# Expert stage of a two-block transformer kernel: all heads of row 0 first, then row 1, each expert choice for one row

## The reference

```
q = (hf @ wq).reshape(t, 8, 2, 128)
sc = einsum('thpd,hpnd->thpn', q, sub_keys)           # 2 x 128 scores for each head
top_v, top_i = top_k(sc, 16)
cand = top_v[:, :, 0, :, None] + top_v[:, :, 1, None, :]    # 16 x 16 candidates
best_v, best_pos = top_k(cand, 16)
expert_id = take_along_axis(top_i0 * 128 + top_i1, best_pos)
gate = softmax(best_v)
# for each token, head and each of the 16 experts chosen:
act = gelu(einsum('phkd,pd->phk', u_table[expert_id], x))
out = einsum('phk,phkd->pd', gate * act, v_table[expert_id])
# then: x = x + out, and a last rmsnorm
```

## Time and profile before

| | us |
|---|---|
| median of 3 runs | 1723.84 |
| the profiled execution | 1718.18 |
| its span in the trace | 1716.9 |
| first gather issued | 1024.46 |
| last gather issued | 1686.90 |
| TensorE / VectorE / ScalarE / GpSimd busy | 1513.6 / 1071.8 / 683.0 / 351.6 |

### The profile page before, as it was taken

The page is one execution under the profiler, slowest core; times in us unless marked ns, Lnnn a source line. Parts: engine busy times, 40 slices in busy tenths (PEclk is TensorE's granted clock), DMA queues, the critical chain, the costliest instruction groups (busy, mean ns, idle before and its releaser), DMA issues.

```text
span 1716.9 us, 21093 instructions
## 1 busy us (share of the span) xinstructions
PE 1513.6 (88%) x7772; PEld 1113.7 (65%) x7772; DVE 1071.8 (62%) x1906; ACT 683.0 (40%) x1512; POOL 351.6 (20%) x325
## 2 busy tenths in 40 slices
PE   3999989998989997998999998788797888887886
PEld 3899988898889997888996774443342434332322
DVE  6666675875665556668454236486776767667645
ACT  2434445344354444643342213334434434343433
POOL 1100010000010001002100013344444444444431
PEclk8999999999999998989999999999999999999999
DMA  9777756664655554332334439989899999999996
GB/s 361 273 246 252 241 189 239 222 204 164 219 170 185 186 187 142 94 97 95 98 99 172 172 104 418 384 318 423 361 422 421 421 422 421 421 421 421 420 422 264
DMA packets 90856, 463.12 MB, mean 270 GB/s; under 512 B 10752, under 2 KB 10912, under 8 KB 57728
## 3 DMA queue, kind: packets, MB, share of 16 engines
q0 software_dynamic: 39216, 277.05, 39.3%
q1 hardware_dynamic: 50688, 183.52, 31.7%
q10 hardware_dynamic: 848, 1.18, 0.2%
HBM read 459.62 MB, written 2.10 MB: 269 GB/s over the span
## 4 chain that ended last, share of the span: by engine, by line
PE 60%; DMA 18%; DVE 13%; ACT 5%; issue 3%; POOL 1%; SPq 0%; DVEq 0%; ACTq 0%; POOLq 0%
DMA Ft<-peer_uv,ids 14%; PE ps L1220 9%; PE ps L460 7%; PE ps L461 7%; PE ps L462 7%; DVE Ft L1982 3%; PE ps L1052 3%; PE ps L1137 3%; PE ps L576 2%; PE ps L577 2%; PE ps L578 2%; DMA mlo<-peer_uv,ids 2%; DVE wlo L1243 2%; PE ps L504 2%; PE ps L505 2%
## 5 line engine op out<-in xcount | busy, mean ns | idle before, releaser
L1220 PE MATMUL ps<-Ft 128*128 128x512 f32 x796 | 385.3, 618 | 81.7 <-ACT Ft L2505 81.1
L1220 PEld LDWEIGHTS ps<-Ft 128*128 128x128 f32 x796 | 145.0, 194 | 306.1 <-ACT Ft L2505 174.6
L1243 DVE TENSOR_TENSOR wlo<-raw,whi 128x1024 fp32r<-128x1024 f32 x228 | 277.9, 1244 | 69.0 <-ACT whi L2006 68.6
L460 PE MATMUL ps<-uhi,whi 128*128 128x256 f32 x1088 | 314.2, 289 | 6.6 <-DVE ulo L1331 6.0
L1982 DVE CUSTOM_DVE_ANT_0 Ft<-Ft 128x1024 f32<-128x1024 f32 x199 | 243.9, 1226 | 116.9 <-DMA Ft<-peer_uv,ids 108.6
L461 PE MATMUL ps<-ulo,whi 128*128 128x256 f32 x1088 | 310.7, 286 | 0.0
L462 PE MATMUL ps<-uhi,wlo 128*128 128x256 f32 x1088 | 310.3, 285 | 0.0
L2627 POOL DMA_INDIRECT Ft<-peer_uv,ids x199 | 221.0, 1111 | 314.4 <-PE ps L1220 241.7
L2006 ACT ACTIVATE whi<-raw 128x1024 fp32r<-128x1024 f32 x228 | 229.7, 1048 | 27.7 <-DMA raw<-ff_gu 15.7
L460 PEld LDWEIGHTS ps<-uhi,whi 128*128 128x128 f32 x1088 | 211.7, 195 | 10.5 <-issue 8.3
L461 PEld LDWEIGHTS ps<-ulo,whi 128*128 128x128 f32 x1088 | 211.6, 194 | 1.9 <-issue 0.5
(11 more groups left out here) (411 smaller groups left out, 2177.1 us busy)
## 6 DMA issues: line engine op xcount, KB each, us to landing
raw<-ff_gu SPq DMA_DIRECT2D x88, 512.0 KB, 4.7
raw<-w_ada SPq DMA_DIRECT2D x72, 512.0 KB, 5.0
raw<-ff_dn SPq DMA_DIRECT2D x44, 512.0 KB, 4.5
raw<-w_in SPq DMA_DIRECT2D x32, 512.0 KB, 3.7
raw<-w_in_s SPq DMA_DIRECT2D x28, 512.0 KB, 4.2
raw<-w_out SPq DMA_DIRECT2D x14, 512.0 KB, 4.6
raw<-w_in_m SPq DMA_DIRECT2D x12, 512.0 KB, 4.6
raw<-xa_wk SPq DMA_DIRECT2D x8, 512.0 KB, 3.6
```

The costliest lines, as they stand in the source:

```text
L460: t.matmul(o, hi[:, c], x[0][:, i], start=(k == 0), stop=False)
L1220: ins = t.matmul(acc[r][c], diag[n % NDIAG], gbuf[n % NGAT][:, 1024 + c * 512:1024 + (c + 1) * 512], start=(hh == 0 and s == 0), stop=(hh ...
L1243: v.tensor_tensor(lo, raw_slot(j), hi.bitcast(F32), ALU.subtract).then_inc(*up("lo", j))
```

## The change

`peer_order` gets another list. There are now sixteen choices, each for one row: choice q is head q % 8 of row q // 8, and pair n belongs to choice n // 16. Each choice is put among the pairs by a formula, and each engine's step of it at a place of its own: tile, pq (the copy of the query), keys, scs (the copy of the scores), six steps of route, and drain. Row 1's attention is also split by engine: out1 behind every third pair from 3 to 24, residuals and squares (res1, sq1), mean1, dgr1, cols1 for TensorE, cols1a for ScalarE, cols1v for VectorE, up to place 62. The last norm of row 0 moves from the last choice to places 137 to 160. The scores have two buffers for row 0 and eight for row 1 (`keyed`), the masks of both halves are made in one operation, and the last norm has a small buffer for each row.

```diff
+    def put(place, *what):
+        side[place].append(what)
+    for q in range(1, 16):
+        p = {2: 1, 8: 64}.get(q, 16 * q - 40)
+        first, each = {1: (0, 1), 2: (16, 1)}.get(q, (16 * q - 24, 2))
+        for k in range(6):
+            put(first + each * k, "route", q)
+        put(first + 6 * each + (5 if each == 1 else 4), "drain", q)
+        if q > 1:
+            put(p, "tile", q)
+            put(p + 4, "pq", q)
+            put(p + 6, "keys", q)
+            put(p + 10, "scs", q)
+    put(1, "turn", 0)
+    put(1, "turn", 1)
+    for k in range(8):
+        put(3 + 3 * k, "out1", k)
+    for n in range(2):
+        put(22 + 12 * n, "res1", n)
+        put(23 + 12 * n, "sq1", n)
+    for place, what in ((40, "mean1"), (52, "dgr1"), (53, "cols1"), (57, "cols1a"), (62, "cols1v")):
+        put(place, what)
+    put(100, "rows", 1)
+    for place, part in ((137, 0), (145, 1), (160, 2)):
+        put(place, "last", 0, part)
+    for what in (("drain", 0), ("tile", 1), ("pq", 1), ("keys", 1), ("scs", 1), ("rows", 0), ("soft",)):
         yield what
...
+    for n in range(256):
+        yield "pair", n, n // 16, n % 16
+        side[n].sort(key=lambda w: w[0] != "drain")
+        yield from side[n]
+    for part in range(3):
         yield "last", 1, part
...
+    keyed = [scs[:, q % 2 * 256:q % 2 * 256 + 256] for q in range(8)] + [m32[0][:, a:a + 256] for a in range(0, 2048, 256)]
...
-            for half in range(2):
-                w3 = grid(wk[:, half * 512:(half + 1) * 512], 32)[:, a * 16:(a + n) * 16, :]
...
+            settle(v, v.tensor_tensor(wk, bc(pf.unsqueeze(2), [128, 32, 16]), bc(iota16.unsqueeze(1), [128, 32, 16]),
+                                      ALU.is_equal), "top", q, "eq")
...
         def choice_k(q):
...
-            if q:
-                a.wait_ge(*at("chosen", q - 1))
...
+            if 2 <= q < 8:
+                a.wait_ge(*at("ids", q - 2))
+            a.activation(keyed[q], spot["pk", q][:, 0:256], ACT.Copy).then_inc(*up("peer_a", "scs", q))
...
+                s.wait_ge(*at("peer_t", "tile", 8 + hh, half))
```

More of the change, by code:

```diff
@@ L171 @@
 T_OUT, T_XQ, T_XO, T_PQ = 0, 8, 16, 24
-CHOICES = [(0, (0,)), (1, (0,)), (0, (1,)), (1, (1,))] + [(hh, (0, 1)) for hh in range(2, 8)]
 def peer_order():
-    for what in (("tile", 1, 0), ("tile", 1, 1), ("keys", 1), ("drain", 0), ("rows", 0), ("soft",)):
-        yield what
[L186 to L208, removed]
@@ L1123, in values, with peer_tile @@
             give(("x_o", r, g), "oTc", r, g)
[L1125 to L1140, removed]
+        def peer_tile(q):
+            r, hh = divmod(q, 8)
+            o = bank(("pq", q))
+            t.wait_ge(*at("xTa", "ffn", r))
+            t.wait_ge(*at("xTv", "ffn", r))
+            for half in range(2):
+                i = T_PQ + 2 * hh + half
+                t.wait_ge(*at(f"tail{i % NTAIL}", i))
+                for k in range(8):
+                    ins = t.matmul(o[:, half * 128:(half + 1) * 128], tail_slot(i)[:, k * 128:(k + 1) * 128],
+                                   fT[:, k, tok(r)], start=(k == 0), stop=(k == 7))
+                ins.then_inc(*up("peer_t", "tile", q, half))
+            give(("pq", q), "peer_a", "pq", q)
         def peer_keys(q):
-            hh, rows_ = CHOICES[q]
+            r, hh = divmod(q, 8)
             o = bank(("pk", q))
@@ L1148, in peer_keys @@
             for half in range(2):
[L1149 to L1152, removed]
+                c = r * 256 + half * 128
+                ins = t.matmul(o[:, half * 128:(half + 1) * 128], pq[:, c:c + 128],
+                               subk[:, (2 * hh + half) * 128:(2 * hh + half + 1) * 128], start=True, stop=True)
             ins.then_inc(*up("peer_t", "pk", q))
-            give(("pk", q), "peer_a", "pk", q)
+            give(("pk", q), "peer_a", "scs", q)
         def run(gen, n=8):
@@ L1207, in peer @@
                     run(out1, 1)
-                elif what == "late" and args[0] == 2:
+                elif what == "cols1":
                     norm_cols("ffn", 1)
@@ L1874, in route @@
         def route(q):
[L1875 to L1878, removed]
+            v.wait_ge(*at("peer_a", "scs", q))
             for half in range(2):
[L1880 to L1883, removed]
@@ L1891, in route @@
[L1891 to L1896, removed]
-            i4 = ixf[:, 64:128].rearrange("p (two r s) -> p two r s", two=2, r=2)
@@ L1943, in peer @@
         def peer():
-            gens = [route(q) for q in range(10)]
+            gens = [route(q) for q in range(16)]
             for what, *args in peer_order():
                 if what == "route":
-                    next(gens[args[0]], None)
+                    next(gens[args[0]])
                 elif what == "drain":
@@ L2619, in gpsimd_engine @@
         first_use = {4: ("q", 1, 1), 5: ("s", 1, 1), 6: ("pT", 1, 1), 7: ("o", 1, 1)}
-        for n, hh, r, s in PAIRS:
-            if s == 0:
-                p.wait_ge(*at("ids", CHOSEN[hh, r]))
+        for n in range(256):
+            if n % 16 == 0:
+                p.wait_ge(*at("ids", n // 16))
             if n >= NGAT:
```

182 lines of the change are left out of this document (81 added, 101 removed).

## The result

The changed kernel takes 1706.18 us in the median of 4 runs (1700.85 to 1709.51), against 1723.60 for the kernel before in the same session. The ratio is 0.9895, with a 95% interval of 0.9869 to 0.9921. The forecast was 1706. In a second session the same two kernels gave 1705.40 and 1721.57, a ratio of 0.9913 (0.9890 to 0.9936).

A forecast was written before the change was run, and what follows sets the result against it. The prediction took the expert stage to be bound by its DMA transfers. Its terms, 20.1 + 0.6 - 2.0 - 1.25 + 0.4 = 17.9 us, taken from 1723.8 gave 1705.9, say 1706 us, with a range of 1702 to 1717.

The forecast's parts named there:

- The bound: Expert stage: bound by its transfers, DMA share 1.01 at 421 GB/s from 1224 to 1696 us.
- The three causes: Late ids of choices 1, 2 and 4 left DMA holes of 2.8, 11.2 and 6.1 us; removing them gains 20.1.
- Choice 0's masks: VectorE ahead of the first gather: three mask operations of 0.69 us replace six of 0.43, gaining 0.6 us.
- The hole at pair 9: TensorE waits 3.3 us for tile 3's weight, so the next gather is about 2 us late: -2.0 us.
- rival D: TensorE's clock stays at 1.2 GHz through the first 25 pairs, giving 1764 us; chance 0.05.
- Row 0's output and the last gather: Row 0's 0.52 MB output moves into the saturated stretch, costing 1.25 us; the last gather gets 0.4 back.
- ScalarE's table loads: 12 more table loads, 15.4 us on ScalarE, fit into its idle time and count 0.
- Choice 1's ids, the first pair: Choice 1's ids come at about 1053 us; the first pair's matmul at 1038.7 instead of 1041.4.
- The signs of being wrong: VectorE waiting over 5 us for ScalarE's copy in 40 pairs, dip over 5 us, or share below 0.95 after 1100.

The follow-up runs named there:

- b_ids1: Kernel before, with only choice 1's route steps moved earlier, behind pairs 0 to 5: stage 690.2 us against 692.4.
- ids_m2: Changed kernel with the ids of choices 3 to 15 behind pair 16q - 2 instead of 16q - 14: 1754.95 us, ratio 1.0204 to the kernel before.
- b_row0_4heads: Kernel before, with four single-row choices of row 0, four of row 1, then four two-row ones, old step table kept in kind: 1736.09 us, ratio 1.0092.
- ids_m7: Changed kernel with the ids of choices 3 to 15 behind pair 16q - 7 instead of 16q - 14: 1706.49 us, stage 677.4.
- ngat8: Changed kernel with eight gather buffers instead of nine: stage 678.5 us in a single run.

## Why the prediction was right, and where it was off

- **The bound, right.** Transfers bind: 421 GB/s over 472 us before and over 604 us after, and halving the bytes cut the stage from 675.4 to 540.1.
- **The three causes (+20.1), right.** No wait for ids is left behind the first, and none of the old holes is there. b_ids1 shows the first alone, at 2.2 us where 2.8 were put down. The second and third were not undone one by one; that they had the size put down is argued from their waits being absent. What ids_m2 adds is that late ids by themselves bring holes back. The order of rows did not do it by itself in b_row0_4heads, where the stage grew by 15.8 us; whether it takes a place for each engine's step or only better places in the old table is open.
- **Choice 0's masks (+0.6), right.** The first gather came 2.02 us later than before (1026.48 against 1024.46) while TensorE's tile ahead of it came 2.67 later: 0.65 us.
- **The hole at pair 9 (-2.0), the right mechanism and too small: this is the step that failed.** Tile 3 stood 39.3 us behind the first gather (38.6 forecast), the load landed after 8.6, the wait was 2.99 (3.3 forecast). "Then come the half (1.8) and pair 9 (1.7)" is the sentence that was wrong. From start to start they took 3.57 and 2.86, 2.9 us more, since the clock had gone to 0.50 during the wait. The hole measured 4.0 to 4.2, and taking the wait away gave 3.0 and 3.4 us of stage. The forecast had weighed the low clock as rival D for 25 pairs or not at all, and never as a price on one wait. Rival D did not come: the clock was back at 0.93 within the 4 us from 1076.

  A second term of the same sum was off the other way. What it has as "about 3 us from issue to its first bytes" was between 1.5 and 1.9: the gather was issued at 1077.54, and the DMA engines moved nothing from 1078 to 1079 and half a full rate's worth in the next microsecond.

```profile
1078.00:1079.00 1.00, 1.00 (x4) 0.52 (x3) 0.96 (x2) 0.19 (x1) 0.48 (x1) 1.00 0.00 0
1079.00:1080.00 1.00, 1.00 (x3) 0.40 (x3) 0.97 (x7) 0.00 (x0) 0.00 (x0) 1.00 0.93 229
```

  So the hole was, it seems, mostly the low clock and hardly the wait. Two comparisons agree on it, each between single profiles: in ids_m7 the two steps took 5.23 us instead of 6.43, and the stage was 1.0 shorter; and the 3.2 us that the stage lost to tile 3 are about the 2.9 that the low clock added. An estimate from these is that the same wait at full clock would have cost a few tenths with nine buffers; no run with nine buffers shows it.
- **Row 0's output and the last gather (-1.25, +0.4), the right sign and too small.** In the last stretch up to the last dot product the transfers lost 9.83 x (1 - 87/421) = 7.8 us, against 9.06 x (1 - 168/421) = 5.4 in the old kernel. That is -2.4, where the net was -0.85. The windows after and before:

```profile
1684.00:1693.83 9.83, 7.91 (x17) 2.68 (x17) 4.93 (x8) 3.59 (x12) 0.00 (x0) 1.00 0.21 87
```

```profile
1696.00:1705.06 9.06, 7.09 (x16) 2.39 (x15) 4.95 (x10) 3.59 (x12) 0.00 (x0) 1.00 0.42 168
```

  The last gather's gain is there: VectorE's last two dot products start 2.46 us apart, against 2.88 in the earlier trace rows:

```profile
1691.37 1.23 DVE L1966 CUSTOM_DVE_ANT_0 Ft<-mlo,Ft 128x1024 f32<-128x1024 f32 x1 [1.24 <-DMA mlo<-peer_uv,ids]
...
1693.83 1.23 DVE L1966 CUSTOM_DVE_ANT_0 Ft<-Ft 128x1024 f32<-128x1024 f32 x1 [1.23 <-DMA Ft<-peer_uv,ids]
```

- **ScalarE's table loads (0), right.** There are 31 loads, at the same 1283 ns as in the earlier trace rows; the DMA share was 1.00 or more in every 20 us from 1080 to 1680:

```profile
L2468 ACT ACT_TABLE_LOAD x16 | 20.5, 1283 | 0.3
L2432 ACT ACT_TABLE_LOAD x15 | 19.2, 1283 | 0.3
```

  The last column is ScalarE's idle time ahead of them, 0.3 us for each group. Behind a load the next operation starts at once:

```profile
1300.79 1.28 ACT L2468 ACT_TABLE_LOAD   x1
1302.08 0.20 ACT L2468 ACTIVATE Ft<-Ft 128x1 f32<-128x1 f32 x1
```

  The Trainium skill, "ScalarE: Activation LUTs", section "What ACT_TABLE_LOAD costs", counts a drain into its 2.66 us; these rows show none.
- **Choice 1's ids, the first pair, right.** The ids came 26.7 us behind the first gather (29 forecast), and the first pair 15.0 (14.8 forecast).
- **The signs of being wrong.** None came: the dip lost 4.0 us and not over 5, no share over 20 us fell below 0.95 from 1100 us to the drain at 1684, and VectorE did not wait for a copy by ScalarE within the first 40 pairs.

Measured by the stage and the start, the change is worth 14.1 + 0.65 = 14.75 us in the profiled pair of executions, against 17.9 forecast. The missing 3.1 us are the hole (2.0 to 2.2), 1.5 at the end, and about 0.5 of crumbs that I can't place (rates that differ by one or two GB/s in the windows between), less 0.9 us that the last norm's output and its tail came out shorter (10.97 us from the last dot product's start to the end of the span, 11.84 before). These come from rounded rates, so each may be off by some tenths. That the median met the forecast to 0.2 us is luck: single executions lie up to 5 us to either side of it, and the time alone would have hidden the error.

## What to carry to other kernels

Where a queue of transfers binds, keep the work that makes its addresses some pairs ahead, and count for every wait put among the first pairs also what TensorE may cost behind it at the lower clock: here a 3 us wait cost 2.9 us more of TensorE's time in three profiles, 1.7 in two and 0.1 in one. Give each engine's share of a step a place of its own, behind what it needs and ahead of who needs it; reordering whole steps moved the holes and made the kernel 0.9% slower. Read a few microseconds from a stage's length between two marks in the trace, not from medians, if what lies ahead of the stage scatters by more.

## What the runs showed of the hardware

- TensorE waited 2.95 to 3.04 us for tile 3's weight in six profiles. The half tile behind it took 3.62 to 3.78 us in five of them and 2.05 in one (ngat8). Pair 9 behind the half was still slow in three (2.97 to 3.02 us: both profiles of the changed kernel, ids_m2) and at full clock in the others (1.88 to 1.90). What decides it stays open.
- A 512 KB load through SyncE's queue landed 8.6 us after issue, while the gathers of the saturated stretch take 17.5 us from issue to landing.
- The transfers tail off before they land. From 1684 to 1693 us the DMA engines moved 94 GB/s, less than one gather's bytes, and yet the last five dot products, the last four of which each waited for their gather, start 2.43 to 2.47 us apart. From 1690 on the share is 0.06, as much as one of the 16 engines busy and the others idle:

```profile
1684.00:1693.00 9.00, 7.57 (x16) 2.50 (x15) 4.93 (x8) 3.02 (x11) 0.00 (x0) 1.00 0.22 94
1691.00:1692.00 1.00, 0.82 (x2) 0.49 (x3) 0.63 (x1) 0.13 (x1) 0.00 (x0) 1.00 0.06 25
```
